# Recurrence of a hybrid trunk: next pair's reciprocals in three parts, the second rate's products one slot later

## What is computed

```python
kk = (k * W['b_kk'][e]).reshape(B, T, B_HEADS, HEAD_DIM)
kk = kk * lax.rsqrt(jnp.sum(kk * kk, axis=-1, keepdims=True) + 1e-12)
wl = W['b_w0'][e, d] + jnp.tanh(wd) @ W['b_w2'][e, d]          # first rate: decay
decay = jnp.exp(-jnp.exp(-jax.nn.softplus(-wl) - 0.5))
a = jax.nn.sigmoid(W['b_a0'][e, d] + ad @ W['b_a2'][e, d])      # second rate
kd = k * (1 + (a - 1) * W['b_ka'][e])
# step: sa = S @ -kk;  S = S * decay + sa (kk * a)^T + v kd^T;  y = S @ r
```

## Time and profile before

| | |
|---|---|
| median of 3 runs | 2892.51 us (2885.69 to 2899.96) |
| the profiled execution | 2893.07 us |
| its span, first to last instruction | 2891.3 us |
| mean granted TensorE clock | 0.955 |
| PE busy, of the span | 2643.5 us (91%) |
| DVE busy, of the span | 1670.6 us (58%) |
| ACT busy, of the span | 1479.3 us (51%) |
| recurrence, in the trace | about 380 to 870 us |

### The profile page before, as it was taken

One profiled execution on the slowest core, in us unless ns is written; L12 is line 12 of the kernel. 1 busy time (PEld: TensorE's weight loads), 2 busy tenths in 40 slices (PEclk: granted clock), 3 DMA queues, 4 the chain that ended last, 5 costly groups with the idle time before them and its releaser, 6 DMA issues. The chain is left out here.

```text
span 2891.3 us, 46735 instructions
## 1 busy us (share of the span) xinstructions
PE 2643.5 (91%) x16147; PEld 2304.6 (80%) x16147; DVE 1670.6 (58%) x2418; ACT 1479.3 (51%) x2317; POOL 383.4 (13%) x523
## 2 busy tenths in 40 slices
PE   6998979999997999998979988886999999999993
PEld 5887868787884888887867778875999999999993
DVE  3355555555546432322241158844888898989896
ACT  4225745554542233331122246632888887878783
POOL 1223111111001400000130034314000000000002
PEclk9998979999998999999989989996999999999997
DMA  7621000000006222213316400033999999999995
GB/s 260 206 99 18 2 5 1 1 1 1 2 1 246 85 73 74 72 44 117 109 44 232 166 29 18 10 113 117 365 386 381 385 381 380 381 380 380 381 380 202
DMA packets 263225, 472.02 MB, mean 163 GB/s; under 512 B 29452, under 2 KB 202636, under 8 KB 256948
## 3 DMA queue, kind: packets, MB, share of 16 engines
q1 hardware_dynamic: 255600, 445.82, 43.7%
q0 software_dynamic: 4416, 14.70, 1.3%
q10 hardware_dynamic: 3076, 9.71, 0.9%
HBM read 453.67 MB, written 16.48 MB: 163 GB/s over the span
## 5 line engine op out<-in xcount | busy, mean ns | idle before, releaser
L3331 DVE TENSOR_TENSOR m_lo<-m_raw,m_hi 128x1408 fp32r<-128x1408 f32 (+1 forms) x459 | 648.5, 1458 | 61.9 <-ACT m_hi L3190 58.7
L3190 ACT ACTIVATE m_hi<-m_raw 128x1408 fp32r<-128x1408 f32 (+1 forms) x459 | 548.4, 1246 | 38.3 <-DMA m_raw<-moe_w_gu 24.4
L213 PE MATMUL acc<-w_hi,h_hi 128*128 128x512 f32 (+1 forms) x1120 | 431.6, 385 | 16.6 <-PEq L2750 7.8
L195 DVE TENSOR_TENSOR w_lo<-w_raw,w_hi 128x1024 fp32r<-128x1024 f32 (+1 forms) x132 | 162.1, 1231 | 484.8 <-ACT w_hi L190 484.0
L215 PE MATMUL acc<-w_hi,h_lo 128*128 128x512 f32 (+1 forms) x1120 | 425.2, 380 | 0.0
L214 PE MATMUL acc<-w_lo,h_hi 128*128 128x512 f32 (+1 forms) x1120 | 424.9, 379 | 0.0
L190 ACT ACTIVATE w_hi<-w_raw 128x1024 fp32r<-128x1024 f32 (+1 forms) x134 | 135.0, 1014 | 457.5 <-PE acc L215 407.4
L213 PEld LDWEIGHTS acc<-w_hi,h_hi 128*128 128x128 f32 x1120 | 213.3, 190 | 78.4 <-issue 33.9
L215 PEld LDWEIGHTS acc<-w_hi,h_lo 128*128 128x128 f32 x1120 | 212.9, 190 | 34.5
L214 PEld LDWEIGHTS acc<-w_lo,h_hi 128*128 128x128 f32 x1120 | 213.1, 190 | 32.5
L3108 PE MATMUL p_gates<-m_hi,x_hi 128*128 128x352 f32 x544 | 181.3, 333 | 5.0 <-DVE m_lo L3331 5.0
(11 more groups left out here) (407 smaller groups left out, 5327.2 us busy)
## 6 DMA issues: line engine op xcount, KB each, us to landing
m_raw<-moe_w_gu SPq DMA_DIRECT2D x544, 352.0 KB
m_raw<-moe_w_dn SPq DMA_DIRECT2D x187, 512.0 KB
ada_w<-ada_w SPq DMA_DIRECT2D x40, 1024.0 KB, 4.8
w_raw<-ffn_w_gu SPq DMA_DIRECT2D x88, 256.0 KB, 2.9
w_raw<-w_in_o SPq DMA_DIRECT2D x24, 512.0 KB, 5.7
w_raw<-ffn_w_dn SPq DMA_DIRECT2D x22, 512.0 KB, 3.5
w_raw<-w_in_e SPq DMA_DIRECT2D x28, 384.0 KB, 4.9
scratch_y_slots<-y_slot ACTq DMA_DIRECT2D x18, 512.0 KB, 6.3
```

The costliest lines, as they stand in the source:

```text
L195: eng.tensor_tensor(lo, self.raw_of(c, k), hi, ALU.subtract).then_inc(self.lo.sem, 1)
L213: eng.matmul(out, hi, whi[:, b, :], start=first, stop=False)
L3190: a.activation(whi[:, u % MSPLIT, 0:size(u)], raw[:, s, 0:size(u)], ACT.Copy).then_inc(s_hi.sem, 1)
L3331: dve.tensor_tensor(wlo[:, u % MSPLIT, 0:n], raw[:, u % MRAW, 0:n], whi[:, u % MSPLIT, 0:n], ALU.subtract).then_inc(s_lo.sem, 1)
```

## The change

The reciprocal of 640 columns is cut into three of 256, 192 and 192 columns, which stand in slots 2, 3 and 4; the product of kk moves to slot 6. The second rate's products and sigmoids move from slots 6 and 20 to slots 7 and 21, so that they stand behind level 0 and `chain_r` of the next step. Other pieces keep their slots. The first pair's reciprocal is also cut in three, one after the other, in `first_dve`. The counts of `s_rs` follow.

```diff
+            ROOTS = ((0, 256), (256, 448), (448, T))
+
+            def root_dve(k):
+                def f(dve, ct):
+                    if k == 0:
+                        dve.wait_ge(s_eps.sem, s_eps.at(2 * ct + 2))
+                    x, y = ROOTS[k]
+                    dve.reciprocal(rs[:, x:y], lw[:, x:y]).then_inc(s_rs.sem, 1)
+                return f
+
             def norm_dve(dve, ct):
-                dve.wait_ge(s_eps.sem, s_eps.at(2 * ct + 2))
-                dve.reciprocal(rs[:], lw[:]).then_inc(s_rs.sem, 1)
-                dve.wait_ge(s_rs.sem, s_rs.at(ct + 1))
+                dve.wait_ge(s_rs.sem, s_rs.at(len(ROOTS) * (ct + 1)))
                 dve.wait_ge(s_raw.sem, s_raw.at(ct + 1))
                 dve.tensor_tensor(kk[:], kk[:], rs[:], ALU.mult).then_inc(s_kk.sem, 1)
...
-                            a.wait_ge(s_rs.sem, s_rs.at(ct + 1))
+                            a.wait_ge(s_rs.sem, s_rs.at(len(ROOTS) * (ct + 1)))
...
-            PREP = [(0, "act", squares_act), (1, "pe", norm_pe), (1, "act", norm_act), (2, "dve", norm_dve)]
+            PREP = [(0, "act", squares_act), (1, "pe", norm_pe), (1, "act", norm_act)]
+            PREP += [(2 + k, "dve", root_dve(k)) for k in range(len(ROOTS))] + [(6, "dve", norm_dve)]
             for d, at in ((0, 5), (1, 19)):
                 PREP += [(at, "pe", lora_pe(d, 0)), (at, "act", lora_act(d, 0)),
-                         (at + 1, "pe", lora_pe(d, 1)), (at + 1, "act", lora_act(d, 1)), (at + 2, "dve", scan_dve(d)),
+                         (at + 2, "pe", lora_pe(d, 1)), (at + 2, "act", lora_act(d, 1)), (at + 2, "dve", scan_dve(d)),
...
-            PAIR_SLOT = (1, 5, 6, 19, 20)
+            PAIR_SLOT = (1, 5, 7, 19, 21)
...
-                dve.reciprocal(kk_root, kk_root).then_inc(s_rs.sem, 1)
-                dve.wait_ge(s_rs.sem, s_rs.at(1))
+                for x, y in ROOTS:
+                    dve.reciprocal(kk_root[:, x:y], kk_root[:, x:y]).then_inc(s_rs.sem, 1)
+                dve.wait_ge(s_rs.sem, s_rs.at(len(ROOTS)))
```

More of the change, by code:

```diff
@@ L2699, in rwkv_stage @@
             s_copied.base += NT + 2
-            for s, n in ((s_raw, 1), (s_sq, 1), (s_prod, 10), (s_eps, 2), (s_rs, 1), (s_kk, 1), (s_sig, 8), (s_scan, 2 * NT),
+            for s, n in ((s_raw, 1), (s_sq, 1), (s_prod, 10), (s_eps, 2), (s_rs, len(ROOTS)), (s_kk, 1), (s_sig, 8), (s_scan, 2 * NT),
                          (s_half, 2), (s_lm, 2), (s_lx, 2), (s_exp, 8), (s_kd, 6), (s_tilde, 8)):
```

## The result

The changed kernel takes 2862.43 us as the median of 4 runs (2861.88 to 2864.87); the kernel before, with one more run than above, takes 2895.80 (2885.69 to 2899.96). The ratio is 0.9878, with a 95% interval of 0.9856 to 0.9899: faster by 1.0 to 1.4%, where 2865 was forecast. The profiled execution took 2861.88 us, 31.2 less than that of before. The medians are 33.4 us apart, since the profiled execution of the kernel before lies 2.7 us under the median of its four.

What follows compares the result with a forecast made beforehand. TensorE on the critical path, held up by two queues and then slowed by half clock, was taken as the bound. Gains of 6.2 + 1.6 + 23.1 - 0.3 = 30.6, less 2.95, took 2893.07 to 2865 us; range 2856 to 2882.

Steps and rivals of the forecast that it cites:

- The stall of the reciprocal: Slots 2 to 4: TensorE's 2.07 us wait for VectorE's reciprocal vanishes at each of three pairs, 6.2 us gained.
- Part A: Reciprocal cut in three: 6.2 us of stall and 1.6 of half clock beside pair 0 gained, 0.3 lost.
- The durations of the parts: VectorE's three reciprocal parts in slots 2 to 4: 1.75, 1.35 and 1.35 us, leaving 0.4 us cover before level 6.
- The 0.3 us lost in the first pair's preparation: First pair's preparation: two extra fixed parts of 0.158 us lie on VectorE's path, 0.3 us lost.
- The wait changes hands: After level 0's squares, transposes wait for ScalarE's copies behind the table load and sigmoids; 0.87 us of standing still remain.
- Part B: Second rate's products one slot later: a pass shrinks from 13.26 to 9.41 us, 3.85 each, 23.1 us for six.
- The sum: Whole kernel, clock held: 6.2 + 1.6 + 23.1 - 0.3 = 30.6 us gained.
- The clock term: Behind the rate passes: the clock falls to half at one pass in six, giving back 2.95 us.
- The clock at every pass: Rival: the clock still falls at all six rate passes, giving back 17.7 us, 2880; chance 0.16, including four or five.
- VectorE as the bound: Rival: reciprocal parts delay additions TensorE wants in slots 2 to 4, so Part A gains nothing, 2873; chance 0.09.
- The longer half clock: Rival: half clock behind each rate pass lasts another 6.7 us, costing 20.1 us over six, 2900; chance 0.04.
- The gain that is absorbed on the way: Rival: later stages absorb the gain or removed waits return one for one, between 2880 and 2893; chance 0.05.

Runs made afterwards that it cites:

- early_table: Changed kernel plus a one-column sigmoid ahead of the first rate's sigmoid waits, so ScalarE loads its table earlier; run three times: medians 2862.92, 2856.02, 2859.18 us.
- longer_stall: Changed kernel plus a one-column Exp between the first rate's products and their sigmoids, a second table load in direction 0 only; 2872.98 us.
- only_roots: Kernel before with only the reciprocal cut in three and the product of kk in slot 6; second rate's products stay in slots 6 and 20; 2884.46 us.
- only_rates: Kernel before with only the second rate's products moved to slots 7 and 21, one reciprocal in slot 2; 2868.33 us.
- one_root: Changed kernel with one reciprocal of 640 columns in slot 2 again, product of kk still in slot 6; 2864.46 us.
- late_part: Changed kernel with reciprocal parts of 128, 128 and 384 columns instead of 256, 192 and 192; 2860.29 us.
- after_again: The changed kernel unaltered, run once more on the same chip beside the third early_table run; 2859.38 us, ratio 0.9869 to the kernel before.
- fill_stall: Kernel before plus four useless 128x256 products between the first and second rate's products, filling TensorE's 1.77 us gap; 2878.45 us.

## Why the prediction was right

**The stall of the reciprocal** is gone, and no other took its place, as laid out. It gave 2.34 us a pair instead of 2.07: without the stall the level-4 product starts 0.99 us after the squares do (508.59 and 509.58), before they have ended, so 3.23 - 0.99 = 2.24 were lost there, and the wait in the row was only the part in which TensorE was idle. The last 0.1 is not explained. Beside pair 0 the clock's share was 1.10 + 0.67 = 1.8 us (1.6 predicted). Part A measured 3 x 2.34 + 1.8 = 8.8 us against 7.8.

**The durations of the parts** were estimated as 1.75 and 1.35 us from two sizes; they are 1.74 and 1.33 to 1.34. Part 3 ended at 519.42, and level 6 began 0.56 us after the additions had ended, where 0.4 was predicted. The 0.3 us lost in the first pair's preparation did not come, as VectorE's timelines of the kernel before and of the changed one show:

```profile
364.81 4.14 DVE L2600 RECIPROCAL x<-x 128x640 f32<-128x640 f32 x1
...
364.25 4.17 DVE L2611 RECIPROCAL x<-x 128x256 f32<-128x256 f32 x3
```

Three parts one behind the other take 4.17 us where the whole took 4.14. The fixed part of 0.158 us is therefore not paid again when the parts follow each other at once: this term was mis-sized, at 0.3 for 0.03.

**The wait changes hands** to ScalarE's queue: 0.87 us predicted, 0.95 measured, six times. early_table shows the cause, the load of the table. By the Trainium skill's drain ("ScalarE: Activation LUTs", What ACT_TABLE_LOAD costs) it would have been 2.25 us, an estimate; the sigmoids began 0.02 us behind the load, and neither here nor in the double load of longer_stall (523.90 + 1.28, sigmoids at 525.19) is there a drain.

**Part B** was forecast at 3.85 us a pass. In direction 0 it is 28.49 - 24.66 = 3.83. The pass itself, up to the level-2 squares, takes 9.41 us as worked out. In direction 1 it is 28.21 - 24.66 = 3.55, because the half clock had cost less there: against the passes of only_roots in which it held (26.0) it cost 2.2 us in direction 1 and 2.5 in direction 0. The working took direction 0 for both. Six passes gave 22.2 us against 23.1.

**The sum is right partly by luck.** With the clock held it was 30.6 us, and the profiled executions differ by 31.2. Part A gave 1.0 more than its term, part B 0.9 less, the first pair's 0.3 was not lost, and 0.2 came from outside the recurrence. The medians differ by 33.4 us, where 27.7 was forecast; 2865 is near the measured 2862.4 because the starting point, 2893.07, lies 2.7 us under the later median of the kernel before.

**The clock term was the wrong step.** I took one fall in six. There was none in the 12 passes of the two profiled executions, nor in the 18 of only_rates, one_root and late_part. It moved the forecast by 2.95 us. A fall measured in whole intervals cost 2.2 to 2.5 us in the kernel before, since later waits absorb some of it, and up to 4.6 elsewhere. The reason given was a shorter stall between wider work. The length is supported by the tally of the profiled executions; that the wider work matters is not shown, since no run has a stall of 0.95 us between narrow products:

| TensorE's standing still | where | clock fell |
|---|---|---|
| 0 to 0.95 us | rates moved (after, after_again, only_rates, one_root, late_part; early_table three times) | 0 of 48 |
| none, gap filled | fill_stall (both rates in their old slots) | 0 of 6 |
| 1.16 to 1.18 us | one_root, longer_stall (direction 1) | 0 of 6 |
| 1.77 us | before / only_roots | 6 of 6 / 2 of 6 |
| 2.07 us | before, only_rates, fill_stall (reciprocal) | 1 of 3 each |
| 2.46 us | longer_stall (direction 0) | 2 of 3 |

**The rivals.** The clock at every pass (2880) did not happen. The Trainium skill ("TensorE: Matmul & The Clock Gate", A second HAM failure mode) describes a clock that swings because TensorE idles briefly but frequently between groups of matmuls, and gives no length for the idling. The changed kernel still idles 0.95 us six times, and its trace shows none of that swinging in the prepared steps (1.00 from 384.9 to 838.8). VectorE as the bound (2873) did not happen; late_part shows that even a wait at level 6 would have been free. The longer half clock does exist, 10 us against 6.7, at 2.46 us of stall and once at 1.77 us in only_roots, but not in the changed kernel. The gain that is absorbed on the way (2880 to 2893) did not happen.

**What stays open.** What decides whether a stall of 1.77 or 2.07 us brings the clock down: in one execution the same stall in the same code did so beside one pair and not beside the next (only_roots, and the reciprocal in three kernels). The rows show lengths and tallies, not the cause. Open too is where the executions of early_table with the lower mean clock lose their 7 us.

## What to carry to other kernels

Price a stall of TensorE by the interval that it lengthens, against an equal interval without it, and not by the idle time in its row: here 1.77 us of idling cost another 2.2 to 2.5 us at half clock behind it, and the quickest way to show it was to fill the gap with useless products. When a wait for one engine is moved away, read the queue of the engine that freed the resource: its instructions are still ahead of what comes next, and that remainder is the new stall. A long instruction of a helper engine that blocks short ones is best cut to the size of the gaps in its queue, and a wait is free as long as a later one, on an input that doesn't move, absorbs it.

## What the runs showed of the hardware that was not expected

GpSimd and VectorE slow each other. al arrives later, so GpSimd's product of al and kk now runs beside VectorE's subtraction L2173 (L2164 before). Both read two inputs. Source lines of the changed kernel, in ns, min/median/max:

```profile
L2165 POOL TENSOR_TENSOR iclr<-iclr,kk x6: 2121/2126/2131, 413.2 to 693.0; 128x640 f32<-128x640 f32 x6
...
L2173 DVE TENSOR_TENSOR L_centred<-L,half_end x3: 1476/1476/1480, 412.4 to 645.6; 128x640 f32<-128x640 f32 x3
```

Before they took 1535 and 819 ns, one after the other. The Trainium skill, "GPSIMD Engine Reference", 1. Specifications, says that the two share their ways into SBUF, with contention when VectorE reads two SBUF inputs; the trace agrees, with 0.66 us on VectorE and 0.59 on GpSimd. The kernel before shows the same in the first pair's preparation, where VectorE's product for zr (L2609) takes 2154 ns beside GpSimd's L2624 and 826 ns elsewhere (L2218). The prediction had no such term. It cost nothing, since L_before still ended at 533.36, and the exponential that waits for it began at 536.05.

A reciprocal that is cut in parts costs nothing more when the parts stand directly behind each other (4.17 us for three, 4.14 for one), though a single one has a fixed part of some 0.16 us (an estimate from 0.189 us for 5 columns and 4.14 for 640).

Four products that nobody needed in each of six gaps made a kernel 16 us faster (fill_stall). And nine executions of one kernel (only_roots) differ by 19 us, with mean granted clocks from 0.960 (the shortest) to 0.952 (the longest). The waits of eight of them were not profiled, so that the clock alone makes the difference is likely but not shown.
